# A transformer layer with expert retrieval: tokens 0 to 255 go ahead, and 177 of their gathered dots move under the other tokens' stages

## What is computed

```python
def reference(x, mem, ...):
    h = layer_norm(x, ln_in_g, ln_in_b)                    # 1024 tokens x 1024
    proj = h @ w_in                                        # gMLP half and chunk-band attention half
    ...
    h = layer_norm(DN_ALPHA * h + mix @ w_out, ln1_g, ln1_b)
    h = layer_norm(DN_ALPHA * h + memory_cross_attention(h, mem, w_xq, w_xk, w_xv, w_xo), ln2_g, ln2_b)
    h = layer_norm(DN_ALPHA * h + peer_ffn(h, w_pq, sub_keys, expert_u, expert_v), ln3_g, ln3_b)
    return h

def peer_ffn(h, w_pq, sub_keys, expert_u, expert_v):
    q = (xf @ w_pq).reshape(t, PEER_HEADS, 2, PEER_HALF)   # 8 heads, two halves
    s = jnp.einsum('thpd,hpkd->thpk', q, sub_keys)         # 128 key scores of each half
    sv, si = lax.top_k(s, PEER_TOPK)                       # 16 best of each half
    gv, gp = lax.top_k(comb, PEER_TOPK)                    # 16 best of the 256 sums
    ...
    def block(args):
        u = expert_u[idx_blk]                              # 128 rows of 16384 for each token
        a = g_blk * jax.nn.gelu(jnp.einsum('tkd,td->tk', u, x_blk))
        return jnp.einsum('tk,tkd->td', a, expert_v[idx_blk])
```

## Time and profile before

| what | value |
|---|---|
| time, median of 3 runs | 3456.94 us (3453.18 to 3470.61) |
| span of the profiled execution | 3451.3 us, 5.6 us under that median |
| stages before the experts (498 to 1226 us) | 728 us |
| phase A, G, B | 994, 306 and 925 us, of B 29 us before its first product |
| TensorE busy | 3047.1 us (88%) |
| VectorE, GpSimd, ScalarE busy | 2172.9, 1466.4, 1137.0 us |
| DMA | 936 MB, 271 GB/s over the span |

### The profile page before, as it was taken

How to read it: one execution, slowest core, us unless ns; L and a number is a source line. 1 busy time by engine, 2 the same in 40 slices (tenths; PEclk the granted TensorE clock), 3 DMA queues, 4 the chain that set the end, 5 groups by cost and what they waited for, 6 DMA issues and landing times. The chain is left out here.

```text
span 3451.3 us, 42749 instructions
## 1 busy us (share of the span) xinstructions
PE 3047.1 (88%) x16184; PEld 2375.8 (69%) x16184; DVE 2172.9 (63%) x4563; ACT 1137.0 (33%) x1747; POOL 1466.4 (42%) x1108
## 2 busy tenths in 40 slices
PE   5996879697879979999999999876749999999996
PEld 4885768587768868787777777654437666676665
DVE  4244774415436758897878876687647666655456
ACT  3213551304221134333333333387612222222222
POOL 3100002300210048876777677687724444424532
PEclk9996799899989989999999999998879999999998
DMA  5333012421422289999999999899999999989992
GB/s 179 114 101 122 1 67 87 140 71 53 140 80 74 62 300 395 395 410 379 410 410 410 403 410 412 345 388 397 406 345 360 372 375 377 351 311 368 381 347 100
DMA packets 371629, 936.06 MB, mean 271 GB/s; under 512 B 32849, under 2 KB 134873, under 8 KB 370401
## 3 DMA queue, kind: packets, MB, share of 16 engines
q0 software_dynamic: 147456, 536.94, 39.8%
q1 hardware_dynamic: 223968, 396.39, 32.1%
HBM read 825.53 MB, written 107.67 MB: 270 GB/s over the span
## 5 line engine op out<-in xcount | busy, mean ns | idle before, releaser
L1654 POOL DMA_INDIRECT ex_ring<-in_expert_v,ex_idxT_sb x405 | 462.8, 1143 | 512.2 <-PE ex_ps_v L1679 224.5
L1654 POOL DMA_INDIRECT ex_ring<-in_expert_u,ex_idx_sb x307 | 399.1, 1300 | 190.3 <-issue 87.5
L110 PE MATMUL eo_ps<-eo_v_hi_sb,aT_late_hi 128*128 128x512 f32 x1024 | 409.1, 400 | 42.2 <-DVE aT_late_lo L2281 42.2
L1663 DVE CUSTOM_DVE_ANT_0 ex_ring<-ex_ring,ex_xg 128x1024 f32<-128x1024 f32 x307 | 368.4, 1221 | 94.3 <-DMA ex_ring<-in_expert_u,ex_idx_sb 92.9
L110 PE MATMUL ex_ps_h<-aT_late_hi,ex_uT_hi_sb 128*128 128x512 f32 x1024 | 413.1, 403 | 1.9 <-ACT ex_uT_lo_sb L1810 1.1
L112 PE MATMUL ex_ps_h<-aT_late_hi,ex_uT_lo_sb 128*128 128x512 f32 x1024 | 402.1, 393 | 0.0
L111 PE MATMUL eo_ps<-eo_v_lo_sb,aT_late_hi 128*128 128x512 f32 x1024 | 401.5, 392 | 0.0
L111 PE MATMUL ex_ps_h<-aT_late_lo,ex_uT_hi_sb 128*128 128x512 f32 x1024 | 400.4, 391 | 0.0
L112 PE MATMUL eo_ps<-eo_v_hi_sb,aT_late_lo 128*128 128x512 f32 x1024 | 400.3, 391 | 0.0
L2289 DVE TENSOR_TENSOR eo_acc<-eo_acc,eo_ps 128x1024 f32<-128x1024 f32 x124 | 151.3, 1221 | 273.2 <-PE eo_ps L112 273.1
L1679 PE MATMUL ex_ps_v<-ex_ring,ex_w_sb 128*32 128x512 f32 x1620 | 233.2, 629 | 82.0 <-DMA ex_ring<-in_expert_v,ex_idxT_sb 66.8
(11 more groups left out here) (368 smaller groups left out, 6424.9 us busy)
## 6 DMA issues: line engine op xcount, KB each, us to landing
ex_u_raw<-in_expert_u SPq DMA_DIRECT2D x128, 512.0 KB, 8.3
eo_v_raw<-in_expert_v SPq DMA_DIRECT2D x124, 512.0 KB, 8.2
act_d<-ex_act SPq DMA_DIRECT2D x128, 256.0 KB, 6.1
gate_d<-ex_gate SPq DMA_DIRECT2D x8, 4096.0 KB, 15.6
eo_g_raw<-gate_d SPq DMA_DIRECT2D x64, 512.0 KB, 8.1
eo_a_raw<-act_d SPq DMA_DIRECT2D x124, 256.0 KB, 6.5
pin_raw<-in_w_in SPq DMA_DIRECT2D x20, 512.0 KB, 4.3
n_row<-h_d SPq DMA_DIRECT2D x16, 512.0 KB, 5.9
```

The source lines that it names most:

```text
L110: pe.matmul(ps, l_hi, r_hi, start=first, stop=False)
L1654: pool.indirect_dma_start(rows(n), None, table, bass.IndirectOffsetOnAxis(at, 0)).then_inc(ring_in[slot[n]], 16)
L1663: dve.tensor_tensor_reduce(out=u, in0=u, in1=xg[:, j, :], scale=1.0, scalar=0.0, op0=ALU.mult, op1=ALU.add, accum_out=hg[:, j, k:k + 1]).t ...
```

## The change

The tokens are split: tiles 0 and 1 (`tiles_a`) pass norm 1, the memory stage, the query projection, the cross attention, norm 2 and the key scores first. Then tiles 2 to 7 (`tiles_b`) pass the same stages again, without the memory stage: its result is written to DRAM (`mk_d`, `mv_d`, 4 MB) in the first cross stage and read back on GpSimd's queue in the second query stage. So `w_out`, `w_xq`, `w_xo` and `w_pq` are loaded and split twice. The key scores of tiles 0 and 1 don't go to DRAM; VectorE ranks them from SBUF in their key score stage, 14 rankings there and the last two in the window.

The five stages of tiles 2 to 7 form a window of 42 steps (class `Window`). In it VectorE first routes tiles 0 and 1, and then makes 177 of their dots, by the table `DOTS` and the `STARTS`; GpSimd issues the gathers, 4 rows ahead at first, 9 ahead from the query stage on. Phase A then makes 303 dots and the values of two whole tiles instead of one (256 rows, from step 8 instead of 40), G is the same in number, and B has no dots and 128 value rows instead of 256.

In the query and key score stages a product row now covers 256 tokens for the first pass, and 256 and 512 for the second (`chunks_b`), where it covered 512 and 512. The copies out of PSUM move there from VectorE to ScalarE.

```diff
+            NORM1, QUERY, CROSS, NORM2, KEYS, STEPS = 0, 6, 14, 20, 26, 42
+            DOTS = [0, 0, 1, 2, 2, 3] + [5] * 8 + [2] * 6 + [4] * 6 + [5] * 16
+            STARTS = {CROSS: 5, NORM2: 4, KEYS: 4}
+            ROUTED = 6
+            @classmethod
+            def dots_by(cls, s):
+                return sum(cls.DOTS[:s + 1]) + sum(n for at, n in cls.STARTS.items() if at <= s)
...
+            def gather_step(self, pool, s):
+                ahead = self.g.FREE if s < self.ROUTED else self.g.FREE + self.g.EARLY
+                if s == self.STEPS - 1:
+                    self.g.gather_to(pool, self.g.issued_by(0))
+                elif s >= 1:
+                    self.g.gather_to(pool, min(self.g.ends[0], self.dots_by(s - 1) + ahead))
...
+                        for to, of in kept or ():
+                            pool.dma_start(to, of.bitcast(F32R)).then_inc(kept_in, 16)
+                        for n in range(0, NB * PIECES, 2):
+                            b, q = divmod(n, PIECES)
+                            pool.wait_ge(hi_done, n + 1)
+                            pool.tensor_tensor(w_lo[:, b % 2, 2 * q:2 * q + 2, :], raw[:, n % 4, :, :],
+                                               w_hi[:, b % 2, 2 * q:2 * q + 2, :], ALU.subtract).then_inc(lo_done[0], 1)
+                            if window and n >= PIECES:
+                                window.gather_step(pool, step + n // 2 - 2)
...
+            def vector_start(self, dve, s, part):
+                if s == self.NORM1 and part == 0:
+                    self.rank_last(dve, 0)
+                if s == self.NORM1 and part == 1:
+                    self.decode(dve, 0)
+                    self.pick_half(dve, 0, 0)
+                    self.pick_half(dve, 0, 1)
+                if part == 0:
+                    self.dots(dve, self.STARTS.get(s, 0))
+            def vector_step(self, dve, s):
+                if s == 0:
+                    self.weights(dve, 0)
+                    self.rank_last(dve, 1)
+                if s == 1:
+                    self.decode(dve, 1)
+                if s == 2:
+                    self.pick_half(dve, 1, 0)
+                if s == 3:
+                    self.pick_half(dve, 1, 1)
+                    self.weights(dve, 1)
...
-            DOTS_A, DOTS_G, DOTS_B = 416, 32, 64
-            VALS_A, VALS_G, VALS_B = P, P, 2 * P
-            WEIGH_A = 40
...
+        DOTS_W, NEAR_W = Window.dots_by(Window.STEPS - 1), Window.dots_by(Window.ROUTED - 1)
+        DOTS_G = 32
+        DOTS_A = GT * P - DOTS_W - DOTS_G
+        VALS_A, VALS_G, VALS_B = 2 * P, P, P
+        WEIGH_A = (6, 73)
...
+        def vals_at(e):
+            for j, (first, last) in enumerate(((WEIGH_A[0] + 2, WEIGH_A[1] - 3), (WEIGH_A[1] + 1, ETILES))):
+                if first <= e < last:
+                    return share(P // 4, last - first, e - first)
+            return 0
+        LAST_VALS, LN_TILES = 116, GROUPS - 2
+        def vals_b(e):
+            return share(P // 4, LAST_VALS - GE, e - GE) if GE <= e < LAST_VALS else 0
...
-        norm_stage("n1", ln1_g, ln1_b, h0_d, h1_d, weight=w_out)
+        tiles_a, tiles_b = range(FIRST), range(FIRST, TT)
+        chunks_a, chunks_b = [slice(0, PAIR)], [slice(PAIR, HALF), slice(HALF, T)]
+        norm_stage("n1a", ln1_g, ln1_b, h0_d, h1_d, w_out, tiles_a)
+        free_sems()
...
         with ExitStack() as memory:
-            msb, _ = local(memory)
-            mk_hi, mk_lo = msb("mk_hi", [P, KT, MEM], F32R), msb("mk_lo", [P, KT, MEM], F32R)
-            mv_hi, mv_lo = msb("mv_hi", [P, MT, D], F32R), msb("mv_lo", [P, MT, D], F32R)
-            memory_stage(mk_hi, mk_lo, mv_hi, mv_lo)
+            tiles = memory_tiles("ma", memory)
+            memory_stage(*tiles)
             free_sems()
-            project_stage("pxq", w_xq, [(xq_d[0:HALF, :], "feat", 1.0), (xq_d[HALF:D, :], "feat", 1.0)])
-            cross_stage(mk_hi, mk_lo, mv_hi, mv_lo)
+            query_stage("qa", chunks_a)
+            free_sems()
+            cross_stage("xa", *tiles, tiles_a, keep=kept(*tiles))
         free_sems()
-        norm_stage("n2", ln2_g, ln2_b, h1_d, h2_d, weight=w_xo)
+        norm_stage("n2a", ln2_g, ln2_b, h1_d, h2_d, w_xo, tiles_a)
         free_sems()
-        key_score_stage()
-        free_sems()
-        early_stack.close()
-        expert_stages(ln3_g, ln3_b, h2_d, out)
-        act_stack.close()
+        with ExitStack() as gathering:
+            g = Gathers(local(gathering, "right")[0], DOTS_W, NEAR_W, planned())
+            with ExitStack() as scratch:
+                window = Window(local(scratch, "right")[0], g)
+                key_score_stage("ka", tiles_a, chunks_a, first=window)
+                free_sems()
+                norm_stage("n1b", ln1_g, ln1_b, h0_d, h1_d, w_out, tiles_b, window, Window.NORM1)
+                free_sems()
+            with ExitStack() as early:
+                g.extras[0] = local(early, "right")[0]("ex_ring_early", [P, g.EARLY, D])
+                with ExitStack() as memory:
+                    tiles = memory_tiles("mb", memory)
+                    query_stage("qb", chunks_b, window, Window.QUERY, kept=kept(*tiles))
+                    free_sems()
+                    cross_stage("xb", *tiles, tiles_b, window, Window.CROSS)
+                free_sems()
+                norm_stage("n2b", ln2_g, ln2_b, h1_d, h2_d, w_xo, tiles_b, window, Window.NORM2)
+                free_sems()
+                key_score_stage("kb", tiles_b, chunks_b, window=window, step=Window.KEYS)
+                free_sems()
+            expert_stages(g, ln3_g, ln3_b, h2_d, out)
```

More of the change, by code:

```diff
@@ L14 @@
+import itertools
 from contextlib import ExitStack
@@ L247, in x, with token @@
                     return row[:, j % ROWS, :]
-                with nc.Block() as block:
+                def token(j):
+                    return slice(tiles[j] * P, (tiles[j] + 1) * P)
+                with nc.Block(no_gpsimd_drain=window is not None) as block:
                     @block.sync
@@ L300, in _ @@
                                 transposed_hi(j - LAG)
-                        for j in range(TT - LAG, TT):
+                            if window:
+                                window.scalar_step(act, step + j)
+                        for j in range(N - LAG, N):
                             transposed_hi(j)
@@ L331, in _ @@
-                        for j in range(TT - LAG, TT):
+                            if window:
+                                window.vector_step(dve, step + j)
+                        for j in range(N - LAG, N):
                             transposed_lo(j)
@@ L1163, in _ @@
+                        if keep:
+                            sp.wait_ge(kept_out, 16 * len(keep))
+                    @block.gpsimd
+                    def _(pool):
+                        for j in range(N):
+                            if window:
+                                window.gather_step(pool, step + j)
                     @block.scalar
@@ L1335, in _ @@
[L1335 to L1337 removed]
+                            if hp // 2 + 1 < NB:
+                                for n in range(2):
+                                    load((hp // 2 + 1) * PIECES + 2 * (hp % 2) + n)
+                            if hp >= 1 and not first:
+                                sp.wait_ge(s_out, hp)
+                                sp.dma_start(s_view[(hp - 1) // 2, (hp - 1) % 2][:, tiles[0]:tiles[-1] + 1, :],
+                                             scores_of(hp - 1)).then_inc(stored[(hp - 1) % 2], 16)
@@ L1339, in _ @@
+                        if not first:
+                            for i in range(2):
+                                sp.wait_ge(stored[i], 16 * (HP // 2))
                     @block.gpsimd
@@ new lines, in planned @@
+        def planned():
+            dots, sums = itertools.count(DOTS_W), itertools.count()
+            parts = []
+            for steps, u, v in ((ETILES, dots_at, vals_at),
+                                (STEPS_G, lambda n: share(DOTS_G, STEPS_G, n), lambda n: share(VALS_G // 4, STEPS_G, n)),
+                                (ETILES, lambda e: 0, vals_b)):
+                part = []
+                for n in range(steps):
+                    part += [("u", next(dots)) for _ in range(u(n))]
+                    part += [("v", next(sums)) for _ in range(4 * v(n))]
+                parts.append(part)
+            return parts
@@ L2234, in _ @@
                         def _(pool):
-                            for n in range(issued_by(END_G), len(gathers)):
-                                gather(pool, n)
+                            g.gather_to(pool, len(g.list))
                             for j in range(TT):
```

1053 lines of the change are left out of this document (606 added, 447 removed).

## The result

The changed kernel takes 3646.13 us (median of 4 runs, 3640.66 to 3666.41) against 3461.28 us for the kernel before: a ratio of 1.0541, 95% interval 1.0499 to 1.0583. It is slower, as forecast, but by more: 3559 us was named, and 3646 lies above the range's end of 3635. The profiled span is 3641.5 us, 190.2 above the 3451.3 of before.

The account below looks back on a forecast made before the run. TensorE was taken to bound phases A and B, with some 30 and 50 us of waits from crowded transfers. Before the experts +140, phase A +54, phase B -92 made +102: 3559 us, range 3490 to 3635.

Parts of the forecast that it names:

- Rivals (1) to (3): Phase A grows by only +20 us: 3434 us (chance 0.07), 3454 us (0.05), or 3499 us with front as forecast (0.18).
- Norm stages, +58: Norms 1 and 2: 46 us for second entries, 4 for dots, 8 for routing; between 46 and 88.
- just covered, I take 4 us: Second norm 2: four dots a tile, some 5.2 us, fit VectorE's 5.7 us idle per tile; 4 us in all.
- Query, +25: Query stages: first pass 36 us, second 79, landings 10, against 100 before; between 12 and 50.
- The term for landings: Second query stage: the last dot's row lands after 7 us, making steps 9.6 us, 10 us in all.
- Cross, +16: Cross stages: a second entry costs 16 us, which no profile row shows; two dots a tile fit under the stage.
- Keys, +41: Key score stages: narrow products +4, second entry +13, VectorE-bound first pass of 98 us +28, less 4; between 17 and 80.
- hidden: Second key score pass: 109 us of dots and some 35 of other VectorE work fit under TensorE's 168 us.
- The prediction's upper end: Key score stages: gathers land late, cover is gone and each step takes their time; up to +80 us.
- The 90 us: Window: VectorE's loss if all 44 GpSimd splits and bias adds held a dot, a third on the path; 3589 us.
- within the edges above: Window: the cost of dots contending with GpSimd's splits and bias adds was taken as inside the stated bounds, without its own term.
- Rival (4): Window: gathers hold weight splits on GpSimd, or TensorE's clock falls; +210, 3667 us, chance 0.13 shared with another rival.

Follow-up runs that it names:

- e1: Changed kernel with no dots in the window, all 177 dots and their gathers back in phase A, routing kept in the window: 3745.84 us.
- e3: Changed kernel with all 177 window dots but about 164 of their gathers left out, so dots reread the same rows: 3577.07 us.
- e2: Changed kernel without window dots, and with the routing of tiles 0 and 1 moved from second norm 1 to second key score stage: 3739.25 us.
- e8: Changed kernel without window dots, routing moved to second key score stage, eight raw weight slots loaded two blocks ahead in query and keys: 3719.16 us.
- e5: Changed kernel with eight raw weight slots instead of four in the query and key score stages, loaded two blocks ahead: 3594.19 us.
- e12: Changed kernel with 139 window dots, fewer at stage ends, eight weight slots loaded two blocks ahead, 4 MB read behind first weight parts: 3565.29 us.
- e6: Changed kernel with two dots a step instead of four in second norm 2, none at its start, none in norm 1: 3601.45 us.

## Why the prediction was wrong, and where it was right

**What bounds the kernel.** Right. TensorE holds A and B at 2.05 us a group: A came out at 1047 (1043 from its first load to its last gelu) where 1048 was named, B at 782 where 785 was. Rivals (1) to (3), in which A absorbs the groups, fell.

**Norm stages, +58, measured +93.** The edges were right: two tiles alone take 47.7 us where 24.3 + 23 makes 47.3, and a bare second entry 95.0 where 96 was worked out. The step that failed is "just covered, I take 4 us" for four dots a tile. It set 5.2 us against the 5.7 us of idle time, as if rows had always landed and no dot met a bias add. It costs 24 us (e1 beside the change): 13 for landings and 11 for dots (e3). Of the 1.4 us that the dots add to a tile, 1.24 are the one dot beside the bias add; four dots without it would just have fitted the idle piece of 4.7 us, as the prediction said. The same stage without dots took 94.1, 97.5 and 95.0 us in e1, e2 and e8, so these figures are good to 3 us. The routing and dots in norm 1 cost 24 where 8 were taken: 13 for the routing (e2), 11 for the dots.

**Query, +25, measured +52.** The step that failed is the first pass: TensorE's time was counted and the supply of weights was not. It takes 49.0 instead of 36 us, and 34.7 when loads are issued earlier (e5). The term for landings took 7 us for a row and 10 in all. A row of the window lands after a median of 6.6 us in e5 (the slots `ex_ring_early`), and the gathers cost 13. That the sum fits is in part luck: in the changed kernel VectorE waits 15 us for rows in this stage, but ScalarE waits 54.5 us for weight parts (37.8 in e1), a path that the term didn't have. By the estimate from the Trainium skill (DMA: Bandwidth & Descriptors, "Anatomy of one DMA — SWDGE (gpsimd) path") a row would land after 3.2 us and the gathers would have cost nothing there; the measurement decides against it. Without gathers the second pass is still 10 us above its 79 (e8). The 4 MB read ahead of the weights is a part of that: in e8 the third and fourth weight parts land 11.0 and 15.9 us after their issue, the first two after 3.1 and 3.3, and the later read of e12 gives back 4 us. The rest is open.

**Cross, +16, measured +28.** Without dots it is +22 (e1). The failed step is the term for the second entry, 16, of which the prediction said that no row shows it; no run takes it apart. The dots with their gathers cost 6, of which e3 gives 3.5 to the dots and 2.5 to the gathers.

**Keys, +41, measured +65.** The first pass was right, 98 named and 98.8 measured. The step that failed is "hidden" for the second pass, 24 us. The dots are hidden (e3: 183.2 us), but the transfers of their rows are not. The prediction's upper end, gathers that land late and hold VectorE, is not what happened: VectorE waits under 10 us for rows, while ScalarE waits 124.7 us for weight parts, which land later beside the gathers. With the parts loaded earlier the second pass takes 186.0 us (e5).

**The collision of VectorE and GpSimd.** It is there: dots beside a bias add take 2.46 us instead of 1.22. The 90 us were too much: in the trace 15 dots of the window overlap GpSimd's adds and splits, and 10 of them are longer, by some 13 us together. But "within the edges above" was too little for norm 2, where such a dot stands in every tile's chain and makes most of what the dots cost. The rule of the Trainium skill (SBUF — State Buffer, "SBUF: two separate sides"), by which the two exclude each other, agrees with the dots that start beside a running bias add (2.46 beside 1.22 us); most of the 44 GpSimd operations met none.

**Rival (4)**, 3667 us, was the nearest in time, though not in all of its mechanism. Gathers hardly held the weight splits on GpSimd: in the changed kernel 21 of its 24 splits in the second query and key stages start 0.1 us behind their high part, and three start 1.0 to 2.2 us behind it. The weights were late from SyncE's queue. The other half of the rival, the clock, is a part of the miss. The granted clock is lower in the thin stages (0.79 to 0.85 of 2.4 GHz, where the earlier trace rows has 0.92 to 0.96). In the first query stage TensorE had stood before its first products; they start 0.21 us apart, at the 1.2 GHz level, and from 618.8 us on 0.12:

```profile
618.01 0.41 PE L117 MATMUL qa_ps<-aT_early_hi,qa_wlo 128*128 128x256 f32 x1
618.22 0.41 PE L115 MATMUL qa_ps<-aT_early_hi,qa_whi 128*128 128x256 f32 x1
...
619.06 0.28 PE L117 MATMUL qa_ps<-aT_early_hi,qa_wlo 128*128 128x256 f32 x1
619.18 0.28 PE L115 MATMUL qa_ps<-aT_early_hi,qa_whi 128*128 128x256 f32 x1
```

Counted over all stages from norm 1 to phase A, 232 products of 256 columns start some 0.21 us apart and 76 of 512 columns some 0.43, which is 37 us more than at the higher level; before it is 35 and 38 products and 11 us. So up to 26 of the 237 us that the stages grew are the clock, as far as no other wait hides them; no run takes it apart from the waits that come before it.

**Open.** Phase A came out at 1043, 1033 and 1023 us in the changed kernel, e6 and e5 (1026 in e3), with no fewer dots or groups; these 20 us are not explained. Nor are 6 of the 10 us of the second query stage, and the second entry of cross.

## What to carry to other kernels

An engine's idle time is a place in its list, not a sum: before work is put "under" it, find the longest single gap per step, and compare it with the work, with what that work costs beside its neighbour on GpSimd, and with its landing. Near the last product of a stage and the first of the next, put only work whose data is sure to be there. When a stage is cut into thinner steps, or other transfers make landings longer, its loads must be issued further ahead, since a landing no longer hides under a step. And a split that loads weights twice pays its edges at every stage: the bare split costs 130 us here (e8; the rankings that make the first key stage longer and a lower clock are in it), more than the 94 that it wins in phase B.

## What the runs showed of the hardware that was not expected

The transfer share of the second key stage rose from 0.84 to 0.94 and ScalarE's wait for weights fell from 124.7 to 10.2 us, with the same loads and gathers: a share of 0.84 with long waits is no sign that bandwidth is short. One slot of 4 KB per partition out of a ring of eight is worth 61 us of phase B. Behind the issue of a 4 MB read on GpSimd's queue, weight parts of 256 KB that SyncE issued landed after 11.0 and 15.9 us, where the two before them took 3.1 and 3.3. A dot that meets a bias add of GpSimd in each tile takes 2.46 us instead of 1.22, and this makes most of the 1.4 us that four dots add to a tile of norm 2.
